# Moving probability and value groups one slot later in the decode attention of a hybrid decoder layer

## What is computed

```
s_s = einsum('bqgrd,bgqnkd->bgrqnk', qb, kv_sel[..., 0, :]) * scale
p_s = masked_softmax(...)                       # selected blocks of 2048 past rows
o_s = einsum('bgrqnk,bgqnkd->bqgrd', p_s, kv_sel[..., 1, :])
s_w = einsum('bqgrd,bkgd->bgrqk', qb, kvw[:, :, 0]) * scale
o_w = einsum('bgrqk,bkgd->bqgrd', masked_softmax(s_w), kvw[:, :, 1])
return gates[..., 0:1] * o_cmp + gates[..., 1:2] * o_sel + gates[..., 2:3] * o_win
```

## Time and profile before

| | before |
|---|---|
| time of three executions | 2768.84, 2774.34, 2776.95 us (median 2774.34) |
| the profiled execution | 2776.95 us, span 2775.1 us |
| busy share of the span | PE 94%, DVE 70%, ACT 38%, POOL 2% |
| chain that ended last | PE 64%, DVE 6%, DMA 2%, issue 2%, ACT 2% |
| in that chain, gather of `sg` from the selected cache | 1% of the span |
| PE line 2235 (MLP) in the chain | 48% of the span |

### The profile page before, as it was taken

How to read it: one execution, slowest core, us unless ns; L and a number is a source line. 1 busy time by engine, 2 the same in 40 slices (tenths; PEclk the granted TensorE clock), 3 DMA queues, 4 the chain that set the end, 5 groups by cost and what they waited for, 6 DMA issues and landing times.

```text
span 2775.1 us, 52028 instructions
## 1 busy us (share of the span) xinstructions
PE 2615.5 (94%) x20033; PEld 2486.9 (90%) x20033; DVE 1956.2 (70%) x3064; ACT 1047.7 (38%) x1311; POOL 51.9 (2%) x106
## 2 busy tenths in 40 slices
PE   8999999997888989976999999999889999999996
PEld 8999999995555669966999999999889999999995
DVE  4688732326763453359888888888778888888897
ACT  3111111116764441135555555555423333333334
POOL 0000000000001100000000000000000000000000
PEclk9999999998999999987999999999999999999998
DMA  8776643316015644323555555555786556655532
GB/s 247 231 231 212 186 76 76 91 32 232 0 76 197 222 159 133 122 62 102 181 191 197 196 185 190 180 180 180 269 290 192 177 177 201 189 185 176 185 112 69
DMA packets 470707, 457.36 MB, mean 165 GB/s; under 512 B 47740, under 2 KB 418644, under 8 KB 459830
## 3 DMA queue, kind: packets, MB, share of 16 engines
q1 hardware_dynamic: 465370, 389.02, 44.4%
q0 software_dynamic: 4608, 67.11, 6.4%
q10 hardware_dynamic: 652, 0.18, 0.0%
HBM read 367.70 MB, written 96.80 MB: 167 GB/s over the span
## 4 chain that ended last, share of the span: by engine, by line
PE 64%; DVE 6%; DMA 2%; issue 2%; ACT 2%; SPq 1%; DVEq 0%; POOL 0%; ACTq 0%; POOLq 0%
PE ps L2235 48%; PE ps L1899 7%; PE ps L2041 1%; PE ps L2152 1%; DMA sg<-in_cache_slc,idx 1%; PE ps L2051 1%; PE ps L2104 1%; DVE pS L1385 1%; PE ps L2065 1%; SPq L526 1%; PE ps L2117 1%; PE ps L2130 1%; DVE y_t L1617 0%; DVE h_t L1617 0%; ACT pS L834 0%
## 5 line engine op out<-in xcount | busy, mean ns | idle before, releaser
L934 ACT ACTIVATE w_sh<-w_s 128x1024 fp32r<-128x1024 f32 (+1 forms) x512 | 473.7, 949 | 818.3 <-PE ps L2235 527.7
L2235 PE MATMUL ps<-h_b,w_sh 128*128 128x288 f32 x3584 | 716.7, 296 | 30.0 <-DVE h_b L1642 21.6
L2235 PE MATMUL ps<-f_b,w_sh 128*128 128x288 f32 x3584 | 717.0, 296 | 21.1 <-DMA f_b<-f_scratch 14.4
L1537 DVE TENSOR_TENSOR w_sl<-w_s,w_sh 128x1024 fp32r<-128x1024 f32 (+1 forms) x512 | 554.4, 1089 | 125.0 <-ACT w_sh L934 124.6
L2235 PEld LDWEIGHTS ps<-h_b,w_sh 128*128 128x128 f32 x3584 | 577.3, 189 | 31.9 <-DVE h_b L1642 14.9
L2235 PEld LDWEIGHTS ps<-f_b,w_sh 128*128 128x128 f32 x3584 | 576.4, 189 | 24.4 <-DMA f_b<-f_scratch 12.6
L2235 PE MATMUL ps<-h_b,w_sl 128*128 128x288 f32 x1792 | 528.5, 295 | 0.0
L2235 PE MATMUL ps<-f_b,w_sl 128*128 128x288 f32 x1792 | 528.3, 295 | 0.0
L738 ACT ACTIVATE w_hi<-w_raw 128x2048 fp32r<-128x2048 f32 x61 | 116.9, 1917 | 615.0 <-PE ps L1899 614.0
L2235 PEld LDWEIGHTS ps<-h_b,w_sl 128*128 128x128 f32 x1792 | 340.6, 190 | 0.0
L2235 PEld LDWEIGHTS ps<-f_b,w_sl 128*128 128x128 f32 x1792 | 340.2, 190 | 0.0
(11 more groups left out here) (272 smaller groups left out, 2622.6 us busy)
## 6 DMA issues: line engine op xcount, KB each, us to landing
w_s<-in_w_mlp SPq DMA_DIRECT2D x512, 256.0 KB, 3.8
f_scratch<-f_st SPq DMA_DIRECT2D x32, 2016.0 KB, 8.9
f_b<-f_scratch SPq DMA_DIRECT2D x56, 1152.0 KB, 8.1
w_raw<-in_w_in SPq DMA_DIRECT2D x90, 512.0 KB, 5.1
x_r<-x_scratch SPq DMA_DIRECT2D x16, 576.0 KB, 5.1
wb<-in_cache_win SPq DMA_DIRECT2D x8, 1024.0 KB, 7.1
w_raw<-in_w_out SPq DMA_DIRECT2D x64, 128.0 KB, 2.9
w_raw<-in_w_out SPq DMA_DIRECT2D x16, 512.0 KB, 4.2
```

The costliest lines, as they stand in the source:

```text
L934: nc.scalar.activation(w_sh[m][:, :, :], blocks, ACT.Copy).then_inc(z_h[m], 1)
L1537: nc.vector.tensor_tensor(w_sl[m][:, :, :], blocks, w_sh[m][:, :, :].bitcast(F32), ALU.subtract).then_inc(z_l[m], 1)
L2235: last = nc.tensor.matmul(ps[:, bank, 0:TH], w[b][:, at_, cols], acts(k, x), start=(start and k == 0 and n == 0), stop=(stop and k == CK - ...
```

## The change

Two lines change. The P turns of the general phases move one slot later, and `s_exp` moves from slot 1 to slot 0 of ScalarE's program (in "last K" too).

```
-P_GROUPS = ((), (), (0, 1, 2), (3, 4), (5,), ())
+P_GROUPS = ((), (), (0,), (1, 2), (3, 4), (5,))
@@ act_phase
                     if k and c < 5:
                         k_copy(*k, c)
-                    if p and c == 1 and place != "last P":
+                    if p and c == 0 and place != "last P":
                         s_exp(*p)
```

## The result

| | before | changed |
|---|---|---|
| median of 5 | 2775.26 us | 2795.80 us |
| lowest, highest | 2768.84, 2777.56 | 2792.81, 2806.50 |
| ratio | 1 | 1.0087, interval 1.0068 to 1.0104 |
| span of the profiled execution | 2775.1 | 2793.1 |

The changed kernel is 20.5 us slower by the medians; by the ratio, which rests on ten executions of it, the loss is 24 us (19 to 29). The forecast was 2790.0 with a range of 2777 to 2802.

What follows compares the result with a forecast made beforehand. One stage (817 to 1016 us) was taken as bound by a nearly closed ring of gather and TensorE work. Steps 11.2, slow clock 3.9 and end 0.6 gave +15.7: 2792.7, or 2790.0 on the median, range 2777 to 2802.

Steps and rivals of the forecast that it cites:

- The ring: P turns and value products, gather overwriting their rows, next K turn: 22.96 of 23.47 us a step, 25.33 after.
- its later issue: In each phase the second gather is issued 12.25 us after P turn 0 instead of 10.56, 1.69 later.
- the landing: Second gather takes 11.0 us from issue instead of 10.0, as the window load overlaps it more.
- The clock: After a longer wait at K turn 2 TensorE runs slow: 1.3 us in three steps of six, +3.9, bounds 0 and +7.8.
- rival B: Contention and slow clock both in full: landing 12.0, slow clock in every step, +25.6, 2800 us; chance 0.18.
- TensorE's own order: Closes a step if gathers land under 7.9 us: 22.2 us a step, −7.0 in all, 2767; chance 0.07.
- the price near +2.0: Upper end of the window load's cost to each second gather's landing, by round-robin queues; the forecast took +1.0.
- no later than the second gather: Sign that the forecast is right: the window load lands no later than the second gather of the phase.
- The waits of 0.34 and 0.88 go: Value product 0's copy wait and the last score product's VectorE wait vanish; TensorE's part falls from 16.06 to 14.84 us.
- P turn 0 at 7.4 if nothing waits: Without DMA waits P turn 0 starts 7.4 us after the phase start, against 7.63 before.
- The last two phases +0.6: End of the stage: an earlier third score product saves 1.4, the weight split ahead of copies 3 and 4 costs 2.0.
- Before the first P turn 0 nothing: Up to the stage's first P turn 0 nothing changes by more than 0.1 us.

Runs made afterwards that it cites:

- e1: Kernel before with the new P-turn group table only, exponential left in ScalarE's slot 1: median 2798.9 us, ratio 1.0076 to the kernel before.
- e2: Kernel before with only the exponential moved to ScalarE's slot 0, old P-turn group table: median 2775.7 us, ratio 1.0006 to the kernel before.
- e5: Changed kernel with gathers of half the bytes (1 MB instead of 2) from the third sequence on: 2769.3 us, one run.
- e4: Changed kernel with the window load issued only after K turn 2, from the third sequence on: median 2786.5 us, ratio 1.0044 to the kernel before.
- e10: Changed kernel with the window load after K turn 2 and 20 extra transpositions ahead of K turn 2: median 2778.7 us, ratio 1.0014 to the kernel before.
- e8: Kernel before with only the window load moved after K turn 2: median 2773.6 us, ratio 0.9995 to the kernel before.
- e7: Changed kernel with 20 extra identity transpositions ahead of K turn 2 in each general phase: median 2786.1 us, ratio 1.0041 to the kernel before.
- e6: Kernel before with gathers of half the bytes from the third sequence on: 2770.9 us, one run.
- e12: Kernel before with only the last P turn moved to slot 5: median 2771.4 us, ratio 0.9997 to the kernel before.
- e9: Kernel before with the last P turn in slot 5 and the window load after K turn 2: median 2769.1 us, ratio 0.998 to the kernel before.
- e11: Kernel before with last P turn in slot 5, window load after K turn 2 and exponential in slot 0: median 2769.9 us, ratio 0.999 to the kernel before.

## Why the prediction was right, step by step

The ring, its later issue and the landing came as forecast. The clock came as in rival B, in every step. With the prediction's own prices this mixture is 11.2 + 7.8 + 0.6 = 19.6, or 2794, and the measured 2795.8 lies nearer to rival B's 2800 than to the 2790.0. That the profiled span fits well (+18.0 against +15.7) is partly luck. The six steps and the end took 24.3 us more where 15.7 were forecast, and 6.3 us came back before the first P turn 0 and behind 1035, where the change does nothing.

- **The ring decides, and a later issue is paid almost in full: right.** The second gather went out 12.2 to 12.8 after P turn 0, forecast 12.25; the excess over 12.25 is in the phases whose P turn 0 still ran at the slow clock. The exponential's place is excluded by e1 and e2, TensorE's own order by e5.
- **The landing grows to 11.0: right, and measured at 11.0.** e4 and e10 show that the window load is the cause. The argument behind it was weaker than the number: I took an upper price from the very first pair of gathers, and e8 shows that the old order paid nothing noticeable for the load. That the middle between 0 and 2.0 was hit is luck. The Trainium skill, "DMA: Bandwidth & Descriptors", section "SWDGE vs HWDGE vs iDMA", has each DMA engine take the two queues in turn. The traces agree in so far as each transfer slowed the other: the window load landed after 9.1 to 10.2 us beside the gather, 6.4 to 7.3 before and 4.9 (median) in e4. They do not bear out the price near +2.0 that I drew from it: it was 0.9 to 1.7. Nor did the load, of half the bytes, get through first: it landed 0.6 to 1.6 us after the gather, and the prediction's sign "no later than the second gather" failed.
- **The slow clock in three steps of six at 1.3: mis-sized.** It came in all six, at 3.65 − 2.08 = 1.6 each. Forecast +3.9, measured about +9.4, and e7 takes 9.7 us off. The bound that I gave (+7.8) had the right count and too small a unit, since in the earlier trace rows only part of K turn 2 and its product was slow. I had estimated a wait of 2 to 3.6 us; it was 2.6 to 4.8, mean 4.0.
- **The waits of 0.34 and 0.88 go: right.** No wait stands before either product. Together they are 1.2 us a step, which is also the difference between e5 and e6.
- **P turn 0 at 7.4 if nothing waits: 0.4 too late** (6.98 in e5), which changes nothing here because the ring decides. The first copy's start was read in a phase whose K turn 0 took 1.50 instead of 1.09.
- **The last two phases +0.6: measured +1.7.** The product behind P turn 0 of "last K" did move from 2.93 to 1.57 after it. The split's slot costs the forecast 2.0 at full clock (e4, e7) and 3.4 in the changed kernel, again by the clock.
- **Before the first P turn 0 nothing: not tellable.** It moved by −5.2 us with the execution and not with the order.

In sum the six steps were forecast at 25.98 (25.33 and 0.65 of clock) and took 27.24. The missing 1.26 × 6 = 7.6 us are in the clock term, of which 5.5 stand directly behind K turn 2 (0.92 × 6) and 1.2 in the later issue; the rest is rounding of the landings.

## What to carry to other kernels

When a buffer is refilled by a transfer that is needed one phase later, write down the ring (last use, issue, landing, first use, back to last use) before moving the last use for the sake of some other wait: covering 1.2 us a phase cost 3.8. Move only the work behind the release. And if a moved transfer meets another one, or a wait on TensorE grows past the ones that the trace has so far, price the overlap and the clock behind the wait separately; they added up here to as much as the delay itself.

## What the runs showed of the hardware

- TensorE's clock after a wait. K turn 2 was wholly or partly at the 1.2 GHz level behind idle times of 2.15, 2.79 (e4), 3.83 (e1) and 3.90 us (changed), and at full speed behind 1.52 (e4), 1.75 (e7, with work ahead of it) and 1.82 (e1). But the length of the wait alone does not tell. Behind 1.97 in e12 the clock was low (granted 0.56 from 884.2 to 887.6), while it was full behind 2.50 (e9) and 2.64 (e1) at K turn 2 and behind 3.30 in e4, at value product 3 of the last phase. What decides between them was not tried.

```profile
884.19 1.59 PE L2104 MATMUL ps<-ident,sg 128*128 128x128 f32 x8 [1.97 <-DMA sg<-in_cache_slc,idx]
885.71 1.98 PE L2117 MATMUL ps<-kT,qb 128*64 128x512 f32 x4
...
1017.24 1.09 PE L2157 MATMUL ps<-sg,sT 128*64 128x128 f32 x16 [3.30 <-ACT sT L890]
```

- Twenty useless transpositions in the wait: with them the granted clock at K turn 2 was 1.00 (e7, 937 to 940), without them 0.50 (changed, 940 to 943), and P turn 0 followed after 2.0 in all six steps instead of 3.3 to 3.8.
- The slow clock also comes where nothing waited that long. In the old order the K turns at a phase's start were slow behind a wait of only 0.88, and with half gathers too (e6). In e8 the K turns at a phase's start took 1.97 and 1.71. What sets it off in these places was not tried.
- Two transfers from different queues, 2 MB gathered and 1 MB plain: with the plain one issued 2.8 us behind the gather, the second gathers of an execution landed after 10.6 to 11.0 us on average (four executions); 5.8 us behind it, after 9.8 to 10.0 (before, e2, e12); after the landing, 9.3 and 9.8 in the new order (e4, e10) and 9.8 to 10.1 in the old (e8, e9, e11). Beside the gather the plain transfer landed after 9.1 to 10.2 us. Half gathers landed in 5.7.
